# Expert tiles in a plain loop of 26 and five rounds of eight, in place of a loop of 16 and fifteen rounds of two

## The reference

```python
def moe(xn, w_router, b_router, w_up, b_up, w_down, b_down):
    logits = (xf @ w_router + b_router).astype(f32)
    top_v, top_i = lax.top_k(logits, TOP_K)          # 4 of 32 experts for each token
    gates = jax.nn.softmax(top_v, axis=-1)
    ...                                              # (token, expert) pairs are sorted by expert, in blocks
    def expert_block(args):
        xblk, e = args
        hmid = xblk @ w_up[e] + b_up[e]              # 1024 -> 2048
        hg = jnp.minimum(hmid[:, :D_FF], SWIGLU_LIMIT)
        hl = jnp.clip(hmid[:, D_FF:], -SWIGLU_LIMIT, SWIGLU_LIMIT)
        act = hg * jax.nn.sigmoid(SWIGLU_ALPHA * hg) * (hl + 1.0)
        return act @ w_down[e] + b_down[e]           # 1024 -> 1024
    ...                                              # times the gate, summed for each token
```

## Time and profile before

| what | value |
|---|---|
| median of 3 runs | 1591.26 us (1591.2 to 1593.9) |
| the profiled execution's own time | 1590.55 us |
| its span | 1588.8 us |
| mean granted TensorE clock | 0.942 of full speed |
| TensorE busy (matmuls) | 1385.0 us, 87% |
| VectorE, ScalarE, GpSimd busy | 638.3, 211.6, 269.0 us |
| HBM traffic over the span | 293 GB/s |

### The profile page before, as it was taken

One profiled execution on the slowest core, in us unless ns is written; L12 is line 12 of the kernel. 1 busy time (PEld: TensorE's weight loads), 2 busy tenths in 40 slices (PEclk: granted clock), 3 DMA queues, 4 the chain that ended last, 5 costly groups with the idle time before them and its releaser, 6 DMA issues.

```text
span 1588.8 us, 33204 instructions
## 1 busy us (share of the span) xinstructions
PE 1385.0 (87%) x12283; PEld 726.2 (46%) x12284; DVE 638.3 (40%) x1434; ACT 211.6 (13%) x561; POOL 269.0 (17%) x322
## 2 busy tenths in 40 slices
PE   7999999989889999779999988795887987876985
PEld 5778777779776443223333332231332332221332
DVE  3999765544562442214242332141222322212222
ACT  2111332413430210000000000000000000000001
POOL 2008600133310011102121111020111111101100
PEclk9999999999999999889999998897898999988998
DMA  8677676212056699999959999999999898999897
GB/s 190 112 174 133 111 130 128 88 47 61 1 181 227 267 403 418 405 418 415 382 239 381 354 387 420 409 396 419 379 361 388 356 362 357 389 399 415 338 373 291
DMA packets 136125, 464.98 MB, mean 293 GB/s; under 512 B 12334, under 2 KB 67254, under 8 KB 103271
## 3 DMA queue, kind: packets, MB, share of 16 engines
q1 hardware_dynamic: 135839, 463.37, 79.8%
q0 software_dynamic: 48, 0.85, 0.1%
q10 hardware_dynamic: 192, 0.13, 0.0%
HBM read 457.84 MB, written 7.34 MB: 293 GB/s over the span
## 4 chain that ended last, share of the span: by engine, by line
PE 63%; DMA 16%; issue 7%; DVE 6%; SPq 4%; POOL 3%; DVEq 1%; ACT 0%; POOLq 0%
PE psum L1244 18%; DMA arena<-in_w_up 15%; PE psum L1256 9%; PE psum L739 8%; PE psum L1212 5%; PE psum L1230 3%; PE psum L1278 3%; DVE acc L1814 2%; PE psum L1131 2%; PE psum L1221 2%; SPq L443 2%; PE psum L1139 2%; PE psum L822 2%; POOL acc L538 2%; SPq L440 1%
## 5 line engine op out<-in xcount | busy, mean ns | idle before, releaser
L1244 PE MATMUL psum<-arena,gate 128*32 128x512 f32 x3264 | 416.0, 644 | 91.3 <-DMA arena<-in_w_up 91.3
L2352 DVE COPY gate<-psum 128x256 f32<-128x256 f32 x51 | 21.6, 424 | 693.3 <-PE psum L1256 693.3
L739 PE MATMUL psum<-arena 128*128 128x304 f32 (+1 forms) x1024 | 263.9, 420 | 4.0 <-DMA arena<-in_w_in 2.5
L1244 PEld LDWEIGHTS psum<-arena,gate 128*32 128x32 f32 x3264 | 100.3, 114 | 365.4 <-issue 266.0
L739 PEld LDWEIGHTS psum<-arena 128*128 128x128 f32 x1024 | 197.1, 193 | 68.1 <-DMA arena<-in_w_in 3.0
L1256 PE MATMUL psum<-arena,gate 128*32 128x256 f32 x3264 | 188.8, 383 | 2.9 <-DMA arena<-in_w_down 1.8
L662 POOL TENSOR_TENSOR qkv<-qkv 128x192 f32<-128x192 f32 x50 | 80.8, 1616 | 605.9 <-DVE qkv L2303 605.9
L1256 PEld LDWEIGHTS psum<-arena,gate 128*32 128x32 f32 x3264 | 101.1, 110 | 86.9 <-issue 22.4
L1814 DVE SCALAR_TENSOR_TENSOR acc<-arena,pcol,acc x240 | 126.4, 607 | 0.1
L1230 PE MATMUL psum<-qkv 128*128 128x512 f32 x102 | 59.7, 669 | 62.9 <-issue 62.4
L1698 ACT ACTIVATE gate<-psum 128x256 f32<-128x256 f32 x51 | 19.6, 383 | 515.1 <-PE psum L1221 515.1
(11 more groups left out here) (429 smaller groups left out, 1315.4 us busy)
## 6 DMA issues: line engine op xcount, KB each, us to landing
arena<-in_w_up SPq DMA_DIRECT2D x256, 1024.0 KB, 10.8
arena<-in_w_down SPq DMA_DIRECT2D x256, 512.0 KB, 8.2
arena<-in_w_in SPq DMA_DIRECT2D x32, 1024.0 KB, 10.6
arena<-in_w_conf_out SPq DMA_DIRECT2D x4, 1024.0 KB, 5.0
arena<-in_state_dn_S SPq DMA_DIRECT2D x8, 512.0 KB, 7.3
arena<-in_w_dn_out SPq DMA_DIRECT2D x1, 4096.0 KB, 14.9
out_ss<-arena SPq DMA_DIRECT2D x8, 512.0 KB, 6.1
arena<-in_w_out SPq DMA_DIRECT2D x1, 4096.0 KB, 16.7
```

Of the source, the lines that this page charges most:

```text
L739: last = mm(bank[2 * (j % 2) + f][:, 0:cols.stop - cols.start], wring[:, slot, k, P * half:P * (half + 1)], rhs[:, k, cols], start=(k == 0 ...
L1244: last = mm(hidden(q)[v], xgT[:, i, SL * q0:SL * (q0 + 1)], parts(wup[k], q)[v], start=False, stop=(k == KC - 1), skip_group_check=True)
```

## The change

`HEAD` goes from 16 to 26. With it `MID` goes from 15 to 5 and `EXTRA` from 3 to 7. The plain loop now does tiles 2 to 25. Each of the five rounds does one tile and then up to seven conditional ones, which are written out in a row, each `If` inside the one before: the first that fails leaves the round.

```diff
@@ -40,7 +40,7 @@
 W = D // G
 XB = ((T - META) * TOPK - NE) // SL
 NT = NE + XB
-HEAD = NE // 2
+HEAD = 26
 NMORE = -(-(T - META) // SL) - 1
 LAST = 1
 MID = NE - HEAD - LAST
...
@@ -1361,14 +1362,15 @@
             spread_choice()
             start_h()
             combine(0)
-            with pe.Fori(2, HEAD) as b:
+            with nc.Fori(2, HEAD, engines=[pe.engine], hint_back_edge=True) as b:
                 tile_step(b)
             nx = pe.value_load(info_i[0:1, 0:1], min_val=0, max_val=XB)
-            with pe.Fori(0, MID) as i:
-                b = pe.value_load(info_i[0:1, bass.ds(i + O_MID, 1)], min_val=0, max_val=XB + MID - 1) + HEAD
+            with nc.Fori(0, MID, engines=[pe.engine], hint_back_edge=True) as i:
+                b = pe.value_load(info_i[0:1, bass.ds(i + O_MID, 1)], min_val=0, max_val=(MID - 1) * (1 + EXTRA)) + HEAD
                 tile_step(b)
-                with pe.Fori(0, EXTRA) as j:
-                    with pe.If(i + j * MID < nx):
+                with ExitStack() as more:
+                    for j in range(EXTRA):
+                        more.enter_context(pe.If(i + j * MID < nx))
                         tile_step(b + j + 1)
             b, prev = nx + (NE - 1), nx + (NE - 2)
             now_in, prev_in = landed_for(b), landed_for(prev)
```

More of the change, by code:

```diff
@@ L671, in _ @@
             selected(1)
-            with pool.Fori(2, HEAD) as b:
+            with nc.Fori(2, HEAD, engines=[pool.engine], hint_back_edge=True) as b:
                 choose(b)
@@ L675, in _ @@
             nx = pool.value_load(info_i[0:1, 0:1], min_val=0, max_val=XB)
-            with pool.Fori(0, MID) as i:
-                b = pool.value_load(info_i[0:1, bass.ds(i + O_MID, 1)], min_val=0, max_val=XB + MID - 1) + HEAD
+            with nc.Fori(0, MID, engines=[pool.engine], hint_back_edge=True) as i:
+                b = pool.value_load(info_i[0:1, bass.ds(i + O_MID, 1)], min_val=0, max_val=(MID - 1) * (1 + EXTRA)) + HEAD
                 choose(b)
                 selected(b)
-                with pool.Fori(0, EXTRA) as j:
-                    with pool.If(i + j * MID < nx):
+                with ExitStack() as more:
+                    for j in range(EXTRA):
+                        more.enter_context(pool.If(i + j * MID < nx))
                         choose(b + j + 1)
@@ L1727, in _ @@
             copy_choice()
-            with act.Fori(2, HEAD) as b:
+            with nc.Fori(2, HEAD, engines=[act.engine], hint_back_edge=True) as b:
                 tile_step(b)
             nx = act.value_load(info_i[0:1, 0:1], min_val=0, max_val=XB)
-            with act.Fori(0, MID) as i:
-                b = act.value_load(info_i[0:1, bass.ds(i + O_MID, 1)], min_val=0, max_val=XB + MID - 1) + HEAD
+            with nc.Fori(0, MID, engines=[act.engine], hint_back_edge=True) as i:
+                b = act.value_load(info_i[0:1, bass.ds(i + O_MID, 1)], min_val=0, max_val=(MID - 1) * (1 + EXTRA)) + HEAD
                 tile_step(b)
-                with act.Fori(0, EXTRA) as j:
-                    with act.If(i + j * MID < nx):
+                with ExitStack() as more:
+                    for j in range(EXTRA):
+                        more.enter_context(act.If(i + j * MID < nx))
                         tile_step(b + j + 1)
@@ L2388, in _ @@
             place_choice(1)
-            with dve.Fori(2, HEAD) as b:
+            with nc.Fori(2, HEAD, engines=[dve.engine], hint_back_edge=True) as b:
                 tile_step(b)
             nx = dve.value_load(info_i[0:1, 0:1], min_val=0, max_val=XB)
-            with dve.Fori(0, MID) as i:
-                b = dve.value_load(info_i[0:1, bass.ds(i + O_MID, 1)], min_val=0, max_val=XB + MID - 1) + HEAD
+            with nc.Fori(0, MID, engines=[dve.engine], hint_back_edge=True) as i:
+                b = dve.value_load(info_i[0:1, bass.ds(i + O_MID, 1)], min_val=0, max_val=(MID - 1) * (1 + EXTRA)) + HEAD
                 tile_step(b)
-                with dve.Fori(0, EXTRA) as j:
-                    with dve.If(i + j * MID < nx):
+                with ExitStack() as more:
+                    for j in range(EXTRA):
+                        more.enter_context(dve.If(i + j * MID < nx))
                         tile_step(b + j + 1)
```

## The result

The changed kernel takes 1610.45 us (median of 4 runs, 1607.32 to 1618.46) against 1591.23 us before: 1.2% slower, ratio 1.0125 with a 95% interval of 1.0087 to 1.0164. I had forecast 1585.3 us and a range that ended at 1606. The profiled execution took 1611.27 us, its span is 1609.5 us, 20.7 more than before's.

What follows compares the result with a forecast made beforehand. TensorE was taken to bound the kernel, with 63% of the chain and 7% issue; 37.8 us goes and 29.6 + 3.0 = 32.6 comes, a gain of 5.2 from 1590.55 to 1585.3 us, range 1564 to 1606.

Steps and rivals of the forecast that it cites:

- The gaps that go: TensorE's issue gaps on the chain from 832 us on, with the slow clock behind them: 37.8 us at most.
- Rival 3: Between tiles: the gaps are worth nothing because the weights' stream fills in; 1590.5 us, chance 0.08.
- The round end without a fetch: End of a round on TensorE with nothing fetched: 1.65 us, or 1.16 over the plain loop.
- the price of a fetch: Instruction fetch at round ends on TensorE: 3.0 us each, two per end, 6.0 us.
- rival 2: At round ends: fetches queue behind weights, stalls are longer, kernel slower; 1602 us at 5 us each, chance 0.33.
- the 3.9 us from which it decides: Price of one fetch at round ends at which what comes, 38.0 us, equals what goes.
- The two ends that should stay hidden: Round ends after tiles 40 and 49: 7.2 us late, covered by a tile that waits for DMA, no cost.
- the 10.7 us of cover: How much later a tile waiting for weights could begin at no cost: 26.8 us to the next start instead of 16.1.
- The hint: One more sequencer instruction per plain iteration, 0.06 us, 1.1 us over 19 boundaries; no time to hide the second fetch.
- Boundaries inside a round: Between conditional tiles in a row: 0.04 us over the plain loop, 14 on the path, 0.5 us.
- the clock: Granted TensorE clock falls behind a stalled round end: 2.7 us lost each, taken between 1.7 and 3.8.
- the exit: Leaving the plain loop on TensorE: stays in the changed kernel, 1.36 us.

Runs made afterwards that it cites:

- The row of three (HEAD = 16): Kernel before with its three conditional tiles written in a row and nested instead of an inner loop, no hints: 1562.76 us, ratio 0.9795.
- the one row without hints: Changed kernel with HEAD = 30, so one round of one tile and 35 conditional ones in a row, prefetch hints taken out: 1560.33 us, ratio 0.9824.

## Why the prediction was wrong

**The gaps that go.** 37.8 us was right in size. The row of three (HEAD = 16) takes away the same gaps and was forecast from the same sum to within 1 us; the kernel with HEAD = 26 and an inner loop came out at 1575 us, where the sum gave 1574. Rival 3, that the weights' stream fills in, is refuted by both. The forecast of 1585.3 starts from the profiled execution; from the median it is 1586.1.

**The round end without a fetch.** 1.65 us, measured 1.62.

**The step that failed: the price of a fetch.** "The fetch has its own queue but shares the engines with the weights, so I take 3.0 us, near the unloaded rows." The count was right: two at each round end with a round behind it, and the 80 packets that I gave for it. The place was right as well, after tiles 30, 35, 40, 45 and 49. The price of 3.0 us holds to 0.3 us without load, where the gaps are near the 7.65 us that I had forecast. Under the weights' stream it is 5.5 us, and the gap 12.67 us on the mean of four. That is rival 2 with its own mechanism, and above the 3.9 us from which it decides: the fetch stands 3.1 to 4.2 us before its packet starts, where 0.5 to 1.5 us do when the weights don't stream. What it waits for there, a queue or the memory, no run tells. With the wrong price the upper end of the range was too low as well: I ended it at 5.6 us, which by the measured price should just have held, if the terms below had not come on top.

**The two ends that should stay hidden.** At 7.2 us late both lay inside the 10.7 us of cover; at 13.4 us the one after tile 40 does not, and its gap of 13.87 us is a piece of the chain, with another 1.6 us of issue inside tile 41. (The cover was read from tile 28. Tile 41's own was 14.7 us, 30.78 us before less a plain tile's 16.1, and the gap, the slow clock and the 1.6 us together exceed that too.) The one after tile 49 is hidden, with 6.80 us: the last round end makes no jump back, so it has one fetch.

**The hint.** 0.06 us a plain iteration was 0.1. "I give it no time to hide the second fetch": it hides 1.3 us. What I did not have at all is its price at the plain loop's exit: the code behind a hinted loop isn't there when the loop ends. That cost tile 26 4.5 us (20.3 against the 15.8 of its neighbour), and 7 us in the kernel before with hints.

**Boundaries inside a round.** I gave them 0.04 us over the plain loop. They are 0.4 us under it, as a tile takes 15.77 us instead of 16.14, 14 times on the path: 5 us in the change's favour.

**The sum again.** Three ends at 12.27 us (the mean of 13.05, 12.94 and 10.81) less 0.49 plus 2.5 for the clock: 42.8 us, where I had 29.6. The entry 4.5, the exit 1.4, the hints 1.9, the end after tile 40 at least the 2.7 us by which 13.4 exceeds 10.7, the boundaries inside rounds 5 the other way. That is 48.3 against 37.8, some 10.5 us slower. The medians say 19.2, the profiled executions 20.7.

More than half of what is missing can be placed, tile by tile, with the one row without hints, which has no gap between tiles 31 and 49. Tiles 40 and 41 take 50.7 us in the changed kernel and 45.5 us there, so the end after tile 40 costs 5.2 us and not 2.7. Tile 44 waits longer for its up weights (31.5 us against 29.2), which makes 2.2 us; whether the late start of tile 41 causes that isn't shown. Another 1.1 us stands before tile 2. The 4 us that are left are spread over pieces of about 1 us or less, which one execution of each kernel can't settle; runs of the changed kernel spread by 11 us.

## What to carry to other kernels

Before a body is written out, count its instructions on each engine, and only those that one pass really runs: on TensorE a loop that ran through nine or more blocks of 16 KB (some 260 instructions each, by the prediction's count) here fetched again at every jump, two stalls of 5.5 us a round, while one of eight or fewer paid nothing after its first visit, and straight code, in a program of 98 packets, paid nothing but one jump at its end. Look also at what the layout asks of the other engines: the table for 35 conditional tiles cost some 5 us on VectorE. A gap that looks large beside a 16 us tile (3 us of branches and register reads) is better removed by the row form inside that limit, or by no loop at all. A price for a fetch taken from transfers on idle queues is too low by almost half where the weights keep the DMA engines busy.

## What the runs showed of the hardware

- A fetch of 16 KB of instructions that TensorE waits for costs 3.3 us with the DMA engines 0.12 busy and 5.5 us at 0.92. The packet itself takes about 1 us, 1.4 us follow it in both cases, and the rest, 0.5 to 1.5 us or 3.1 to 4.2 us, is before it.
- TensorE kept eight blocks of 16 KB: rounds that ran through eight brought none again (HEAD = 22), rounds of nine brought all nine each time (HEAD = 24).
- A prefetch hint on a loop's back edge keeps the code behind the loop from being fetched ahead: the first tile behind it took 20.3 to 23.2 us with the hint, at four places (HEAD = 16, 24, 26 and 30), and 15.6 to 16.2 without, but 17.8 once, where the clock had fallen. With HEAD = 22 a wait for weights hides the stall, and with the DMA engines nearly idle that tile took 17.3 us. The hint hid just 1.3 us of the back edge it named, where that was entered by a jump to just ahead of it.
- A tile's boundary costs 0.49 us in a loop, 0.59 in a hinted loop and nothing in straight code: 16.1, 16.2 and 15.6 us a tile. The sequencer needs 2.1 us from a hinted loop's branch to the next tile's first matmul and 1.7 us from the branch of an `If` that falls through (tiles 9 and 32 of the changed kernel), and the last tile's matmuls still run for some 1.6 us of either.
- The length of a gap did not decide by itself whether the granted clock fell. It fell behind gaps of 1.81 us (HEAD = 22, tile 32, 0.90 over the tile), 1.84 us (the inner loop with HEAD = 26, tile 26, 0.90) and 2.48 us. It did not behind 1.85, 2.32 and once 3.12 us in the kernel before (1.00). Where it fell, the next tile lost 1.7 us behind 3.2 us, 1.8 behind 8.54, and 1.5 to 2.8 behind gaps of 10.6 to 15.0 us, so the clock's part hardly grows with the gap.
